# A transformer step with sixteen experts: the last three experts' rows added by one-hot products instead of the last two, and the halves of x read back, added and normalised earlier and tile by tile

## The reference, cut to what matters

```python
x = x + gate1 * jnp.dot(mix, lp['w_out'])
h = rms_norm(x, lp['norm2_g']) * (1 + scale2) + shift2
return x + gate2 * grouped_moe(h, ...)

# grouped_moe: each token has 2 of 16 experts, both in one group of 4
gates = jnp.sum(jax.nn.one_hot(e_idx, N_EXPERTS) * w_sel[..., None], axis=1)
hid = silu(einsum('td,edf->tef', t, w_gate)) * einsum('td,edf->tef', t, w_up)
hid = hid * gates[..., None]
return einsum('tef,efd->td', hid, w_down)
```

## Time and profile before

| what | value |
|---|---|
| median of three runs | 1267.97 us (1267.76 to 1270.27) |
| the profiled execution | 1267.41 us, its span 1265.6 us |
| TensorE products busy | 1124.1 us, 89% of the span |
| VectorE, ScalarE, GpSimd busy | 885.7, 657.2, 260.6 us |
| chain that ended last | TensorE 68%, VectorE 21%, DMA 6% |
| HBM read, written | 313.40 MB, 26.49 MB; 269 GB/s over the span |

### The profile page before, as it was taken

One profiled execution on the slowest core, in us unless ns is written; L12 is line 12 of the kernel. 1 busy time (PEld: TensorE's weight loads), 2 busy tenths in 40 slices (PEclk: granted clock), 3 DMA queues, 4 the chain that ended last, 5 costly groups with the idle time before them and its releaser, 6 DMA issues.

```text
span 1265.6 us, 15809 instructions
## 1 busy us (share of the span) xinstructions
PE 1124.1 (89%) x6066; PEld 915.6 (72%) x6066; DVE 885.7 (70%) x1111; ACT 657.2 (52%) x908; POOL 260.6 (21%) x220
## 2 busy tenths in 40 slices
PE   5999989989599999999968998788959999999974
PEld 2787757778478888888747876567847888888853
DVE  1138187633679999898853667871379999989884
ACT  2222244431277888888722124442237788888860
POOL 5001111110204212221233021101021322211142
PEclk9999988969799999999978997797969999999997
DMA  9965775740589999999922321014358999999951
GB/s 360 307 227 197 311 313 200 289 176 32 187 319 359 368 390 377 374 379 393 376 121 81 122 75 65 4 40 166 125 213 320 366 384 367 376 379 379 374 207 50
DMA packets 54461, 321.06 MB, mean 254 GB/s; under 512 B 11700, under 2 KB 11812, under 8 KB 19184
## 3 DMA queue, kind: packets, MB, share of 16 engines
q1 hardware_dynamic: 38448, 276.59, 57.3%
q0 software_dynamic: 15936, 43.43, 9.3%
HBM read 313.40 MB, written 26.49 MB: 269 GB/s over the span
## 4 chain that ended last, share of the span: by engine, by line
PE 68%; DVE 21%; DMA 6%; issue 3%; ACT 1%; POOL 0%; SPq 0%; DVEq 0%; POOLq 0%; ACTq 0%
PE bank L1110 34%; PE bank L810 10%; PE bank L1023 6%; DVE w_lo L2095 5%; PE bank L799 4%; DMA ring<-wring_dram 3%; DVE conv_acc L1891 3%; PE bank L916 2%; PE bank L1102 2%; PE bank L888 2%; PE bank L821 1%; DMA y<-y_rows 1%; PE bank L902 1%; DVE rowmax L1691 1%; PE bank L854 1%
## 5 line engine op out<-in xcount | busy, mean ns | idle before, releaser
L2095 DVE TENSOR_TENSOR w_lo<-ring,w_hi 128x2048 fp32r<-128x2048 f32 x190 | 431.9, 2289 | 46.3 <-ACT w_hi L1409 45.8
L1409 ACT CAST w_hi<-ring 128x2048 fp32r<-128x2048 f32 x192 | 367.3, 1918 | 37.4 <-PE bank L1110 37.3
L1110 PE MATMUL bank<-w_hi,hgT_hi 128*128 128x512 f32 x512 | 205.1, 401 | 5.2 <-issue 3.4
L1110 PE MATMUL bank<-w_hi,hgT_lo 128*128 128x512 f32 x512 | 202.0, 394 | 0.0
L1110 PE MATMUL bank<-w_lo,hgT_hi 128*128 128x512 f32 x512 | 201.4, 393 | 0.0
L810 PE MATMUL bank<-ring,hT 128*128 128x256 f32 (+1 forms) x672 | 140.7, 370 | 0.1
L810 PEld LDWEIGHTS bank<-ring,hT 128*128 128x128 f32 x672 | 122.4, 191 | 16.6 <-issue 2.1
L713 POOL DMA_INDIRECT y_rows<-y,y_at x28 | 49.5, 1769 | 387.2 <-ACT y L1439 352.0
L1110 PE MATMUL bank<-w_hi,hidT_hi 128*128 128x512 f32 x256 | 105.4, 412 | 13.5 <-DVE y_lo L2172 13.5
L1110 PEld LDWEIGHTS bank<-w_hi,hgT_hi 128*128 128x128 f32 x512 | 97.5, 190 | 26.5 <-issue 7.2
L1110 PEld LDWEIGHTS bank<-w_hi,hgT_lo 128*128 128x128 f32 x512 | 97.3, 190 | 21.2
(11 more groups left out here) (268 smaller groups left out, 1588.1 us busy)
## 6 DMA issues: line engine op xcount, KB each, us to landing
ring<-wring_dram SPq DMA_DIRECT2D x260, 1024.0 KB, 7.5
y_rows<-hg POOLq DMA_DIRECT2D x6, 1024.0 KB, 7.2
kT<-mod_dram POOLq DMA_DIRECT2D x4, 1024.0 KB, 7.6
late<-y_rows POOLq DMA_DIRECT2D x4, 1024.0 KB, 7.9
ring<-wring_dram SPq DMA_DIRECT2D x6, 640.0 KB, 6.2
h_rows<-h_tok POOLq DMA_DIRECT2D x6, 512.0 KB, 3.0
bias<-na_bias_dram POOLq DMA_DIRECT2D x32, 64.0 KB, 5.5
A<-mod_dram POOLq DMA_DIRECT2D x2, 1024.0 KB, 5.0
```

The lines of the kernel that those rows point to most:

```text
L1110: mm = pe.matmul(b[:, :], a, w[m], start=(start and k == 0), stop=(stop and k == 2))
L1409: act.copy(w_hi[:, q, :], in_ring(l, expert_slot(e, i))).then_inc(hi_made[q], 1)
L2095: dve.tensor_tensor(w_lo[:, q, :], in_ring(l, expert_slot(e, i)), w_hi[:, q, :], ALU.subtract) \
```

## The change

Three edits. (1) `LAST` is 3: experts 13, 14 and 15 go by one-hot products, their turned one-hots in banks 7, 5 and 6, and the lists become 10 to 12 and 13 to 15. Expert 13's split rows are made inside the loop, in expert 14's pass. (2) The read-backs follow expert 12's scatter. ScalarE scales tiles 0 and 1 ahead of expert 15's last two weight slots, VectorE weighs tile 0 inside expert 14's pass and tiles 1 and 2 ahead of the last splits, and GpSimd adds tile 0 ahead of its subtraction. (3) In layer 0 VectorE normalises a tile as soon as its two halves are added, between the additions of the next.

```diff
-LISTS = [range(0, 2), range(2, 6), range(6, 10), range(10, 14), range(14, NE)]
+LISTS = [range(0, 2), range(2, 6), range(6, 10), range(10, 13), range(13, NE)]
-LAST = 2
+LAST = 3
...
-BANK_OF = {"G": 0, "U": 1, "T": 2, "Y0": 3, "Y1": 4, "X0": 5, "X1": 6, "list": 7, "turned": 7,
+BANK_OF = {"G": 0, "U": 1, "T": 2, "Y0": 3, "Y1": 4, "X0": 5, "X1": 6, "list": 7, "turned0": 7, "turned1": 5, "turned2": 6,
...
-        y_hi = nc.alloc_sbuf_tensor_at("y_hi", [P, LAST, D_MODEL], F32R, offset=lent[0])
+        y_split = [nc.alloc_sbuf_tensor_at("y_split0", [P, 2, D_MODEL], F32R, offset=lent[0])]
...
@@ gpsimd, behind the scatters
-                for i in range(2):
-                    pool.wait_ge(y_stored[i], 16 * (NE - LAST) // 2 * (n + 1))
+                for e in (NE - LAST - 2, NE - LAST - 1):
+                    pool.wait_ge(*stored(l, e))
...
+                add_part(0)
+
+                pool.wait_ge(*once_hi(l, NE - 1, 5))
+                q = split_turn(l, NE - 1, 5)[0]
+                pool.tensor_tensor(w_lo[:, q, :], in_ring(l, expert_slot(NE - 1, 5)), w_hi[:, q, :], ALU.subtract) \
+                    .then_inc(lo_made[q], 1)
+
+                add_part(1)
+                add_part(2)
...
@@ tensor, add_last
-                        for part in (y_hi, y_lo):
-                            mm = pe.matmul(bank[bank_no(l, key)][:, :], turned_hot[:, i, t, :], part[:, i, 512 * q:512 * (q + 1)],
-                                           start=(i == 0 and part is y_hi), stop=(i == LAST - 1 and part is y_lo))
+                        for k in range(2):
+                            mm = pe.matmul(bank[bank_no(l, key)][:, :], turned_hot[i][:, t, :], y_split[i][:, k, 512 * q:512 * (q + 1)],
+                                           start=((i, k) == (0, 0)), stop=((i, k) == (LAST - 1, 1)))
...
@@ scalar
+                def y_high(i):
+
+                    act.wait_ge(sems["index_ready"], nth(l, "index_ready", len(LISTS)))
+                    if i == 2:
+                        act.wait_ge(sems["x_part"], nth(l, "x_part", 1))
+                    for m in range(2):
...
+                for e in range(NE - 1):
+
+                    if 0 < e <= NE - LAST:
                         evac_y(e - 1)
+                    elif e:
+                        y_high(e - 1 - (NE - LAST))
...
+                act.wait_ge(sems["weighed"], nth(l, "weighed", 1))
+                scale_part(0)
+                scale_part(1)
                 split_high(NE - 1, 4)
                 split_high(NE - 1, 5)
-                act.wait_ge(sems["weighed"], nth(l, "weighed", 1))
-                scale_part(0)
                 hidden_high(NE - 1)
                 for i in range(LAST):
                     evac_hot(i)
-                scale_part(1)
                 scale_part(2)
-                act.wait_ge(sems["index_ready"], nth(l, "index_ready", len(LISTS)))
-                for i in range(LAST):
-                    y_high(i)
+                y_high(1)
+                y_high(2)
...
@@ vector
                     hidden_rest(e)
+                    if e == NE - 2:
+                        y_rest(0)
                     split_rest(e, 5)
+                    if e == NE - 2:
+                        weigh_part(0)
...
                 hidden_rest(NE - 1)
-                weigh_part(0)
                 weigh_part(1)
-                y_rest(0)
+                weigh_part(2)
                 y_rest(1)
-                weigh_part(2)
+                y_rest(2)
...
+                    add_last(0, 0)
+                    add_last(0, 1)
+                    add_last(1, 0)
                     mean_square(following, "norm1", 0)
-                    add_last(2)
+                    add_last(1, 1)
                     normalise(following, 0)
+                    add_last(2, 0)
                     mean_square(following, "norm1", 1)
+                    add_last(2, 1)
                     normalise(following, 1)
+                    modulate(following, 0)
                     mean_square(following, "norm1", 2)
-                    modulate(following, 0)
                     normalise(following, 2)
```

More of the change, by code:

```diff
@@ L227, in expert_order @@
         order += [("Y0", e), ("Y1", e)]
-    order += [("turned", i) for i in range(LAST)]
+    order += [(f"turned{i}",) for i in range(LAST)]
     order += [(f"A{t}{q}",) for t in range(TILES) for q in range(2)]
@@ L374, in build @@
         chosen_b = overlay("chosen_b", BF16, P, TILES * NE)
+        turned_hot = [nc.alloc_sbuf_tensor_at("turned_hot0", [P, TILES, P], F32R, offset=lent[0])]
         wr_gain = overlay("wr_gain", F32, P, 2, KC, NE)
@@ L394, in build @@
         hgT_hi, hgT_lo = (overlay(n, F32R, P, KC, P) for n in ("hgT_hi", "hgT_lo"))
-        turned_hot = nc.alloc_sbuf_tensor_at("turned_hot", [P, LAST, TILES, P], F32R, offset=lent[0])
+        turned_hot += [nc.alloc_sbuf_tensor_at(f"turned_hot{i}", [P, TILES, P], F32R, offset=lent[0] + 4 * TOK * (i - 1))
+                       for i in range(1, LAST)]
         sg = overlay("sg", F32, P, 2, FF)
@@ L461, in build, with stored @@
         N_CONST = 16 * 8
+        def stored(l, e):
+            return y_stored[e % 2], 16 * (l.n * len(range(e % 2, NE - LAST, 2)) + e // 2 + 1)
         def nth(l, name, k):
@@ L724, in _, with add_part @@
                 extra = pool.value_load(extra_i[0:1, 0:1], min_val=0, max_val=PASSES - 1)
-                pool.wait_ge(*once_hi(l, NE - 1, 5))
-                q = split_turn(l, NE - 1, 5)[0]
-                pool.tensor_tensor(w_lo[:, q, :], in_ring(l, expert_slot(NE - 1, 5)), w_hi[:, q, :], ALU.subtract) \
-                    .then_inc(lo_made[q], 1)
-                for t in range(TILES):
+                def add_part(t):
                     pool.wait_ge(sems["part_weighed"], nth(l, "part_weighed", t + 1))
@@ L1431, in evac_y @@
                 def evac_y(e):
-                    turn = (n * (NE - LAST) + e) // 2
-                    if turn:
-                        act.wait_ge(y_stored[e % 2], 16 * turn)
+                    if e >= 2:
+                        act.wait_ge(*stored(l, e - 2))
+                    elif n:
+                        act.wait_ge(*stored(Layer(n - 1), NE - LAST - 1 - (NE - LAST - 1 - e) % 2))
                     for m in range(2):
@@ L2131, in _, with weigh_part, y_rest @@
                 split_rest(1, 2)
+                def weigh_part(t):
+                    part = parts[t][:, 0, :]
+                    dve.wait_ge(sems["parts_scaled"], nth(l, "parts_scaled", t + 1))
+                    ins = dve.scalar_tensor_tensor(part, parts[t][:, 1, :], gate[:, 1, t:t + 1], part, ALU.mult, ALU.add)
+                    if t < TILES - 1:
+                        ins.then_inc(sems["dve_step"], 1)
+                        dve.wait_ge(sems["dve_step"], step(l))
+                        dve.wait_ge(sems["gate2_loaded"], nth(l, "gate2_loaded", 16))
+                        ins = dve.tensor_tensor(part, part, G[:, min(t, 1), :], ALU.mult)
+                    ins.then_inc(sems["part_weighed"], 1)
+                def y_rest(i):
+                    for m in range(2):
+                        dve.wait_ge(sems["y_hi_made"], nth(l, "y_hi_made", 2 * i + m + 1))
+                        b = bank[bank_no(l, (f"Y{m}", NE - LAST + i))]
+                        half = slice(m * 512, (m + 1) * 512)
+                        dve.scalar_tensor_tensor(y_split[i][:, 1, half], b[:, :], gate_slot[:, i:i + 1], y_split[i][:, 0, half],
+                                                 ALU.mult, ALU.subtract) \
+                            .then_inc(bank_read[bank_no(l, (f"Y{m}", NE - LAST + i))], 1)
                 for e in range(NE - 1):
@@ L2153, in _ @@
                         crowds(l)
-                def weigh_part(t):
-                    part = parts[t][:, 0, :]
-                    dve.wait_ge(sems["parts_scaled"], nth(l, "parts_scaled", t + 1))
-                    ins = dve.scalar_tensor_tensor(part, parts[t][:, 1, :], gate[:, 1, t:t + 1], part, ALU.mult, ALU.add)
-                    if t < TILES - 1:
-                        ins.then_inc(sems["dve_step"], 1)
-                        dve.wait_ge(sems["dve_step"], step(l))
-                        dve.wait_ge(sems["gate2_loaded"], nth(l, "gate2_loaded", 16))
-                        ins = dve.tensor_tensor(part, part, G[:, min(t, 1), :], ALU.mult)
-                    ins.then_inc(sems["part_weighed"], 1)
-                def y_rest(i):
-                    for m in range(2):
-                        dve.wait_ge(sems["y_hi_made"], nth(l, "y_hi_made", 2 * i + m + 1))
-                        b = bank[bank_no(l, (f"Y{m}", NE - LAST + i))]
-                        half = slice(m * 512, (m + 1) * 512)
-                        dve.scalar_tensor_tensor(y_lo[:, i, half], b[:, :], gate_slot[:, i:i + 1], y_hi[:, i, half],
-                                                 ALU.mult, ALU.subtract) \
-                            .then_inc(bank_read[bank_no(l, (f"Y{m}", NE - LAST + i))], 1)
```

(4 more changed lines are left out.)

77 lines of the change are left out of this document (36 added, 41 removed).

## The result

| | before | after |
|---|---|---|
| median of 7 runs each, us | 1270.31 (1267.76 to 1271.87) | 1256.81 (1250.19 to 1262.56) |
| profiled execution, us | 1267.41 | 1256.00 |
| its span, us | 1265.6 | 1254.2 |
| ratio | | 0.9893, 95% interval 0.987 to 0.9916 |

The account below looks back on a forecast made before the run. TensorE's products bound the middle; at layer ends it waits on late halves and VectorE/GpSimd turns. Gains 8.0 (layer 0) + 3.0 (layer 1) + 0.6 (lists) = 11.6 us, from 1267.97 to 1256.4; own range 1252 to 1260, 8-in-10 range 1250.5 to 1262.

Parts of the forecast that it names:

- Read-back one expert earlier: End of each layer: halves issued near 607.5, landing about 616 to 625, so ScalarE's waits go; cost nothing.
- the cover of 5 us: Six-slot weight ring: one expert of 17.7 us, less 9 for landing and some 3.5 of ScalarE reading ahead.
- The estimate by the Trainium skill: DMA queues take turns by packet: half of some 400 GB/s goes to the halves, in by 624; sum stays 1256.4.
- halves come late: Rival, layer 0: weights served first, tile 0's half lands near 629, down products start 647.5; time 1260; chance 0.12.
- one of the signs by which the prediction would have called itself wrong: End of the layer: a wait of ScalarE on a DMA at its scalings of the halves; no size given.
- Turns: VectorE and GpSimd alternate whole SBUF instructions before expert 15's down products: 2.5 us gained in layer 0, 0.8 lost in layer 1.
- the walk: Instruction-by-instruction queue of VectorE and GpSimd at layer end: expert 15's down products start at 643.8, in layer 1 at 1234.8.
- The tail: From expert 15's down products on: unstretched additions start 9.6 us later and take 8.7; 3.0 us gained in layer 1.
- x tile by tile: End of layer 0: tiles normalised between final additions, second projections at 670.5 against 678.5; 8.0 us, containing the 2.5.
- The lists: Fourth list has experts 10 to 12, so TensorE waits less for VectorE's one-hots: 0.3 us per layer, 0.6 in all.
- The clock rival: TensorE stays at the lower clock after 9.3 us of rest, through down products and additions: 18.6 us, 1275; chance 0.05.

Follow-up runs that it names:

- late_read: The changed kernel with its read-back put back to the late place, until expert 15's first product slot and gates are loaded; 1266.33 us, ratio 0.9991.
- vector_subtracts: The changed kernel, but VectorE instead of GpSimd makes the rest of expert 15's weight slot 5, ahead of tile 1's half; 1255.20 us, ratio 0.9892.
- add0_behind: The changed kernel with GpSimd's addition for tile 0 moved behind its subtraction of expert 15's slot 5; 1261.61 us, ratio 0.9947.
- no_norm: The changed kernel without edit 3: layer 0's final additions and normalisings in their old order; 1257.87 us, ratio 0.9912.
- the two experiments: The kernel before with edit 3 alone, 1269.73 us, ratio 0.9999; and the changed kernel without edit 3, 1257.87 us, ratio 0.9912.
- best2: As best, but VectorE also makes slot 5's rest and tile 2's gate product, so GpSimd only adds; 1246.25 us, ratio 0.9828.
- best: Changed kernel; VectorE does expert 14's rests before tiles 1 and 2, expert 15's hidden products before tile 0; ScalarE scales tile 1 later; 1245.89 us, ratio 0.9817.

## Why the prediction was right, step by step

*Read-back one expert earlier: cost nothing.* Right in its worth, wrong in its times. The issue came at 608.38 (forecast 607.5). The halves landed at about 620.5, at 628.6 and at 635.9 instead of 616 for the first and 624 to 625 for the last, and the weight slots beside them took 13.0 us (median, 608 to 640) instead of the 8.3 of the earlier trace rows; the cover of 5 us beyond 8.7 was used almost up, but no split waited for the ring. The last half took 26 us. The 8.3 us from which the prediction took that neither side was starved was one single slot, issued at 630.4, five us behind the read-backs. The estimate by the Trainium skill, page "DMA: Bandwidth & Descriptors", section "Queues, rings and completion order" (all halves in by 624), does not agree with this: 3 MB in 27.5 us (608.4 to 635.9) are some 115 GB/s of about 390, not half. The step that failed is the one from packets to bytes. In this stretch the profile counts 816 packets for the 3.15 MB of GpSimd's queue and 1360 for the 9.42 MB of SyncE's, 3.9 and 6.9 KB each. An estimate from these sizes, a packet each in turn, is 36% or about 140 GB/s, and still lies above the 115. The rival *halves come late* came half true. ScalarE waited 3.12 us for tile 1's half, so its split ended at 631.6, and VectorE waited 1.28 us for it: one of the signs by which the prediction would have called itself wrong. But GpSimd's addition held VectorE's subtraction until 632.2 anyway (629.79 + 2.38), so almost nothing was lost, and layer 1, where ScalarE waited only 1.94 us, starts at the same 44.01. The margin was 0.6 us (631.6 against 632.2), and behind it nothing covers: in late_read halves that land some 9 us later cost all of the gain.

*Turns.* Right. VectorE's steps fell within 0.3 us of the walk: rest of slot 4 done at 634.25 (forecast 634.1), tile 1's first step at 639.8 (639.6), tile 2's step done at 642.2 (642.1), TensorE at 643.81 (643.8). The scatter came 0.42 us later than in the trace of before, so part of this closeness is luck: from the scatter layer 0 gained 2.9 (forecast 2.5) and layer 1 lost 0.4 (0.8). That GpSimd is the cause, and not the half, is shown by vector_subtracts (4.93 to 1.28) and by add0_behind, where the stretch only changed its place. The Trainium skill, page "SBUF — State Buffer", section "SBUF: two separate sides", says that an instruction of VectorE with two SBUF inputs and one of GpSimd that reads SBUF exclude each other for their whole length, whichever starts first. All meetings here agree with it (4.93 behind GpSimd, 1.28 without it).

*The tail.* Additions began 9.46 us after the start (forecast 9.6), unstretched, and with luck: in no_norm, with the same instructions up to there, they began 10.24 us after it, because the clock came back later; six halves took 8.7 us plus what edit 3 puts between them. Layer 1 from start to end: 18.10 us (18.1). Layer 1 gained 3.4 (forecast 3.0).

*x tile by tile.* The sum was right (8.3 us at the second projections for 8.0: 2.9 at the start, 2.0 up to the additions, 3.4 from there to the second projections), the reason partly not. Additions to second projections took 17.36 (forecast 17.1, with the lower clock 17.7). The prediction counted the removed stretch of 2.1 us in layer 0 under the tail and didn't say how little was left for edit 3: the two experiments put it at 0.8 to 0.9 us, and alone it gains nothing by the next scatter, where its 0.6 us of the projections are gone again.

*The lists.* TensorE's wait fell from 1.02 to 0.57 us in layer 0 and from 1.02 to 0.61 in layer 1: 0.4 per layer for 0.3. Layer 1's lies inside the 8.3 us between the scatters. TensorE in time, after:

```profile
408.40 0.38 PE L1084 MATMUL bank<-row_v,one_hot 128*128 128x3 bf16 x9 [0.57 <-DVE one_hot L2081]
```

*The clock rival.* After 9.47 us of rest the products ran at 0.54 for 3.2 us and at 1.00 from 647 on, no longer than the 5 us at 0.50 after a rest of 5.00 us. It fell. But how long the lower level lasts is not settled by this trace: after a rest of 9.45 us in layer 1 of late_read it lasted 6.1 us and put the additions 1.0 us later.

What the prediction didn't ask was whether VectorE's order behind `hidden_rest` was good. The rests of expert 14 release TensorE, the halves of tiles 1 and 2 only the final additions 10 us later. Changing their places gained 21 us against before by the traces (11.9 in layer 0, 9.3 in layer 1), 9.4 us more than the change itself (9.6 by the medians).

## What to carry to other kernels

When a transfer is moved earlier, ask which in-order queue was sitting on it: the gain here came from ScalarE and VectorE reaching the rows that free TensorE, and it ended where the next item of that queue stood. In such a queue, put what releases the bounding engine ahead of what only feeds the end. Between VectorE and GpSimd count the sum of the two times whenever both work in SBUF: moving a GpSimd instruction moves the stretch, and only removing the meeting removes it.

## What the runs showed of the hardware

- Read-backs of 1 MB on GpSimd's queue, issued within 1.5 us beside the weight loads, landed 15.8 (median of two) and 26.0 us after their issue, and the weight slots of that stretch took 13.0 instead of 8.7. DMA view of after, 608 to 640 (first packets, MB and share of the 16 engines of SyncE's queue, `q1`, and GpSimd's, `q0`; then what, queue, count, KB, median us to landing):

```profile
q1 hardware_dynamic: 1360, 9.42, 71.8%
q0 software_dynamic: 816, 3.15, 25.5%
...
ring<-wring_dram SPq DMA_DIRECT2D x7, 1024.0 KB, 13.0
late<-y_rows POOLq DMA_DIRECT2D x2, 1024.0 KB, 15.8
...
y<-y_rows POOLq DMA_DIRECT2D x1, 1024.0 KB, 26.0
```

- VectorE's scalar_tensor_tensor on two SBUF operands is held behind GpSimd too (4.93 and 5.35 us for 1.28), the same instruction on a PSUM bank is not (1.40 us for two, beside GpSimd in the earlier trace rows).
- How long TensorE ran at the lower clock after a rest didn't follow the rest's length. After 9.45 to 9.47 us of rest, ahead of the same down products, the granted clock stayed at 0.50 for 2.9 us (changed kernel, layer 0), 4.0 (its layer 1), 4.6 (no_norm, layer 0) and 6.1 us (late_read, layer 1); after 5.00 us for 4.7 (before), after 3.06 for 6 (best2, layer 1). The fall, too, can come late: in best TensorE rests 1.80 us ahead of expert 15's down products in both layers; in layer 0 the clock fell 0.7 us after they had begun and stayed down for 3.5 us, in layer 1 it didn't fall.
